# First two weight block sums of the 7-product down-projection tiles: by a plain and an adding transfer in place of VectorE

## The reference

```python
def squared_relu_mlp(n, w_up, w_down):
    return jnp.square(jax.nn.relu(n @ w_up)) @ w_down
```

## Time and profile before

| | us |
|---|---|
| median of 3 runs | 946.07 (945.78 to 946.14) |
| the profiled execution, whole | 946.75 |
| its span, first to last instruction | 944.8 |
| TensorE busy | 935.6 |
| VectorE busy | 712.6 |
| ScalarE busy | 595.3 |
| GpSimd busy | 36.2 |

### The profile page before, as it was taken

How to read it: one execution, slowest core, us unless ns; L and a number is a source line. 1 busy time by engine, 2 the same in 40 slices (tenths; PEclk the granted TensorE clock), 3 DMA queues, 4 the chain that set the end, 5 groups by cost and what they waited for, 6 DMA issues and landing times.

```text
span 944.8 us, 14583 instructions
## 1 busy us (share of the span) xinstructions
PE 935.6 (99%) x5944; PEld 832.5 (88%) x5944; DVE 712.6 (75%) x1037; ACT 595.3 (63%) x869; POOL 36.2 (4%) x15
## 2 busy tenths in 40 slices
PE   8999999999999999999999999999999999999997
PEld 7888888888888888888888888999999999999886
DVE  4997747777988867747777988876468789898643
ACT  7676548888655658838888655734555596555532
POOL 0011250000000000020000000000000000000000
PEclk9999999999999999999999999999999999999999
DMA  8554235555565552535554565454544436555541
GB/s 300 222 183 173 91 134 179 183 200 197 181 220 192 178 209 91 178 136 182 191 207 179 183 218 205 163 191 166 179 165 161 166 134 246 179 179 184 193 158 44
DMA packets 25345, 168.22 MB, mean 178 GB/s; under 512 B 2816, under 2 KB 3904, under 8 KB 5568
## 3 DMA queue, kind: packets, MB, share of 16 engines
q1 hardware_dynamic: 24848, 166.84, 49.5%
q10 hardware_dynamic: 432, 0.46, 0.2%
HBM read 166.24 MB, written 1.05 MB: 177 GB/s over the span
## 4 chain that ended last, share of the span: by engine, by line
PE 94%; DVE 3%; ACT 1%; DMA 1%; issue 1%; SPq 0%; DVEq 0%
PE bank L724 23%; PE bank L725 23%; PE bank L726 23%; PE bank L833 12%; PE bank L837 6%; PE bank L752 1%; DMA raw<-w_stream 1%; DVE wlo L1997 0%; PE bank L887 0%; PE bank L1106 0%; PE bank L891 0%; PE bank L895 0%; PE bank L1240 0%; PE bank L1132 0%; PE bank L1114 0%
## 5 line engine op out<-in xcount | busy, mean ns | idle before, releaser
L1997 DVE TENSOR_TENSOR wlo<-raw,whi 128x2048 fp32r<-128x2048 f32 (+2 forms) x133 | 296.8, 2232 | 131.2 <-ACT whi L1340 131.0
L1340 ACT ACTIVATE whi<-raw 128x2048 fp32r<-128x2048 f32 (+1 forms) x139 | 264.7, 1905 | 100.2 <-PE bank L726 97.7
L833 PE MATMUL bank<-nhl,whi 128*128 128x512 f32 x512 | 124.0, 392 | 0.0
L833 PEld LDWEIGHTS bank<-nhl,whi 128*128 128x128 f32 x512 | 94.0, 188 | 18.8 <-issue 0.7
L724 PE MATMUL bank<-mhi,whi 128*128 128x258 f32 x384 | 108.5, 282 | 0.1
L725 PE MATMUL bank<-mlo,whi 128*128 128x258 f32 x384 | 108.3, 282 | 0.0
L726 PE MATMUL bank<-mhi,wlo 128*128 128x258 f32 x384 | 108.2, 282 | 0.0
L724 PE MATMUL bank<-nhl,whi 128*128 128x258 f32 (+3 forms) x320 | 92.2, 288 | 0.0
L725 PE MATMUL bank<-nhl,whi 128*128 128x258 f32 (+3 forms) x320 | 91.4, 286 | 0.0
L726 PE MATMUL bank<-nhl,wlo 128*128 128x258 f32 (+3 forms) x320 | 90.5, 283 | 0.0
L724 PEld LDWEIGHTS bank<-mhi,whi 128*128 128x128 f32 x384 | 72.5, 189 | 0.4 <-issue 0.2
(11 more groups left out here) (389 smaller groups left out, 1914.3 us busy)
## 6 DMA issues: line engine op xcount, KB each, us to landing
raw<-w_stream SPq DMA_DIRECT2D x154, 1024.0 KB, 4.8
h<-x_rows SPq DMA_DIRECT2D x4, 256.0 KB, 5.1
raw<-w_stream SPq DMA_DIRECT2D x2, 512.0 KB, 6.7
cst<-consts SPq DMA_DIRECT2D x1, 832.0 KB, 6.3
e<-g_post SPq DMA_DIRECT2D x1, 512.0 KB, 6.7
out_rows<-e SPq DMA_DIRECT2D x2, 256.0 KB, 2.0
raw<-w_stream SPq DMA_DIRECT2D x1, 352.0 KB, 10.0
vec<-vectors SPq DMA_DIRECT2D x1, 258.5 KB, 9.5
```

The lines of the kernel that those rows point to most:

```text
L833: return pe.matmul(us[c].t[:, :], w[:, k, c * P:c * P + P].hi, nboth[:, k, :], start=k == 0, stop=k == 7)
L1340: act.activation(whi[j][:, 0:n], raw[j][:, 0:n], ACT.Copy).then_inc(s_hi.up(i))
L1997: dve.tensor_tensor(wlo[j][:, 0:m], raw[j][:, 0:m], whi[j][:, 0:m].bitcast(F32), ALU.subtract).then_inc(s_lod.up(i))
```

## The change

The first two weight sums no longer come from VectorE. SyncE issues two plain transfers of B12 (256 KB each, HBM to SBUF) into both halves of the tile, and when they have landed GpSimd issues one transfer of 512 KB (B11 and B22) that adds to what stands there (`accum_op=ALU.add`). So the tile holds B11 + B12 and B12 + B22, where it was B12 - B11 and B22 - B12. The other signs are made up for: in the two adds of `combined` into the second tile, in two of the row sums, and in `seven_2` at the end, each a subtract for an add or the reverse. The number and shape of VectorE's other instructions and all matmuls stay.

The tile of the first two sums is now double: fills q = 0, 2, 4, 6 go to the place of `inval` and `gmask` in `cst`, fills q = 1, 3, 5 to the old `TX[0]`. The second tile, `T24`, stays single. A fill of q >= 2 may start when the sums of q - 2 have been read (`s_ts` and TL's part 0); that of q = 0 waits for the first up-projection bank, that of q = 1 for the last. SyncE does the two plain transfers (`right_block`) just ahead of the stage of the same weight tile (for q = 1, just behind it). GpSimd's adding transfers (`block_sums`) stand in its loop over the tiles. `combined` on VectorE and `combined_hi` on ScalarE wait for their landing (`t13_ready`).

```diff
-        TX = [at(f"tr{i}", 1024, o_nhl + 4096 * i) for i in range(2)]
+        o_inval = CST["inval"][0]
+        T13 = [cst[:, o_inval:o_inval + 1024], at("tr0", 1024, o_nhl)]
+        T24 = at("tr1", 1024, o_nhl + 4096)
...
+        def fill(l, q):
+            return len(SEVEN[q % 2::2]) * l + q // 2 + 1
+
+        def t13_ready(l, q):
+            return s_t13[q % 2], 16 * fill(l, q)
+
+        def t_sums(l, q):
+            return T13[q % 2], T24
...
-                    on.wait_ge(*s_ts.at(l, q, part))
+                    on.wait_ge(*(s_ts.at(l, q) if part else t13_ready(l, q)))
...
-                    act.activation(TH[part], TX[part], ACT.Copy).then_inc(s_thi.up(l, q, part))
+                    act.activation(TH[part], t_sums(l, q)[part], ACT.Copy).then_inc(s_thi.up(l, q, part))
...
             def combined(l, it):
                 q, i = SEVEN.index(it), DOWN[l] + it
-                r = raw[i % NSLOT]
-                right, above = r.rearrange("p (k c n) -> p k c n", k=2, c=2)[:, :, 1, :], r[:, 0:1024].rearrange("p (k n) -> p k n", k=2)
+                r, t1 = raw[i % NSLOT], t_sums(l, q)[0][:, 0:512]
                 on.wait_ge(s_raw[i % NSLOT], 16 * (i // NSLOT + 1))
+                on.wait_ge(*t13_ready(l, q))
                 if q:
                     on.wait_ge(*s_tlo.at(l, q - 1, 1))
-                dve.tensor_tensor(TX[0].rearrange("p (k n) -> p k n", k=2), right, above, ALU.subtract).then_inc(s_ts.up(l, q, 0))
-                on.wait_ge(*s_ts.at(l, q, 0))
-                dve.tensor_tensor(TX[1][:, 0:512], r[:, 1536:2048], TX[0][:, 0:512], ALU.subtract).then_inc(own.up())
+                dve.tensor_tensor(T24[:, 0:512], r[:, 1536:2048], t1, ALU.add).then_inc(own.up())
                 on.wait_ge(*own.last())
-                dve.tensor_tensor(TX[1][:, 512:1024], r[:, 1024:1536], TX[1][:, 0:512], ALU.subtract).then_inc(s_ts.up(l, q, 1))
+                dve.tensor_tensor(T24[:, 512:1024], r[:, 1024:1536], T24[:, 0:512], ALU.add).then_inc(s_ts.up(l, q))
...
-                dve.tensor_tensor(EX[3], EX[1], p5.t[:, :], ALU.add).then_inc(s_ex.up(l))
-                dve.tensor_tensor(EX[0], EX[2], p5.t[:, :], ALU.add).then_inc(p5.free)
+                dve.tensor_tensor(EX[3], p5.t[:, :], EX[1], ALU.subtract).then_inc(s_ex.up(l))
+                dve.tensor_tensor(EX[0], p5.t[:, :], EX[2], ALU.subtract).then_inc(p5.free)
...
-                    dve.tensor_tensor(s1, a21, a22, ALU.add).then_inc(own.up())
+                    dve.tensor_tensor(s1, a21, a22, ALU.subtract).then_inc(own.up())
...
-                    dve.tensor_tensor(s4, a12, s2, ALU.subtract).then_inc(s_as.up(l, q))
+                    dve.tensor_tensor(s4, a12, s2, ALU.add).then_inc(s_as.up(l, q))
...
+            def block_sums(l, q):
+                t = t_sums(l, q)[0].rearrange("p (k n) -> p k n", k=2)
+                i = DOWN[l] + SEVEN[q]
+                corner = W[starts[i]:starts[i + 1]].rearrange("(p k n) -> p k n", p=P, k=4)[:, 0:4:3, :]
+                on.wait_ge(s_t12[q % 2], 32 * fill(l, q))
+                pool.dma_start(t, corner, accum_op=ALU.add).then_inc(s_t13[q % 2], 16)
...
+                if seven_at(i):
+                    block_sums(*seven_at(i))
...
+            def right_block(l, q):
+                t = t_sums(l, q)[0].rearrange("p (k n) -> p k n", k=2)
+                i = DOWN[l] + SEVEN[q]
+                b = W[starts[i]:starts[i + 1]].rearrange("(p n) -> p n", p=P)
+                if q < 2:
+                    on.wait_ge(*use["up", l, 15 * q, q].done())
+                else:
+                    on.wait_ge(*s_ts.at(l, q - 2))
+                    on.wait_ge(*s_tlo.at(l, q - 2, 0))
+                for k in range(2):
+                    sp.dma_start(t[:, k, :], b[:, 512:1024]).then_inc(s_t12[q % 2], 16)
...
+                if i - 1 in (DOWN[0] + SEVEN[1], DOWN[1] + SEVEN[1]):
+                    right_block(*seven_at(i - 1))
+                if seven_at(i) and seven_at(i)[1] != 1:
+                    right_block(*seven_at(i))
```

More of the change, by code:

```diff
@@ L682, in block_kernel @@
         s_as, s_ashi, s_aslo = (sig(n, grid(2, len(SEVEN))) for n in ("as", "ashi", "aslo"))
-        s_ts, s_thi, s_tlo = (sig(n, grid(2, len(SEVEN), 2)) for n in ("ts", "thi", "tlo"))
+        s_ts = sig("ts", grid(2, len(SEVEN)))
+        s_thi, s_tlo = (sig(n, grid(2, len(SEVEN), 2)) for n in ("thi", "tlo"))
+        s_t12, s_t13 = ([sem(f"s_{n}_{i}") for i in range(2)] for n in ("t12", "t13"))
+        def fill(l, q):
[4 more added lines that the diff above has]
+            return T13[q % 2], T24
         s_ex = sig("ex", range(2))
@@ L2341, in combined_lo @@
                     on.wait_ge(*s_thi.at(l, q, part))
-                    dve.tensor_tensor(TL[part], TX[part], TH[part].bitcast(F32), ALU.subtract).then_inc(s_tlo.up(l, q, part))
+                    dve.tensor_tensor(TL[part], t_sums(l, q)[part], TH[part].bitcast(F32), ALU.subtract).then_inc(s_tlo.up(l, q, part))
             def down_lo(l, it):
@@ L2869, in stage @@
                         if seven_at(i - NSLOT):
-                            on.wait_ge(*s_ts.at(*seven_at(i - NSLOT), 1))
+                            on.wait_ge(*s_ts.at(*seven_at(i - NSLOT)))
                         if cuts[i - NSLOT]:
```

## The result

| | before | after |
|---|---|---|
| median of the runs beside each other | 946.0 us (945.51 to 946.38, 6 runs) | 962.71 us (961.07 to 964.18, 6 runs) |
| the profiled execution, whole | 946.75 | 961.07 |
| its span | 944.8 | 959.2 |
| VectorE busy | 712.6 | 693.8 |

The ratio is 1.0175, with a 95% interval of 1.0164 to 1.0186: the kernel became 1.75% slower. The forecast, 946.1 us and a range up to 952.0, was wrong. The profiled execution of the changed kernel is the fastest of its six, 1.6 us under their median.

The account below looks back on a forecast made before the run. TensorE was taken as the bound, busy 935.6 of 944.8 us, so VectorE's relief gains 0 and every added transfer cost is 0: 946.75 + 0 profiled, 946.1 us on the median's scale; 8-in-10 range 945.3 to 952.0 us.

Parts of the forecast that it names:

- Bound and gain: Down-projections: TensorE never waits, so taking 17.1 us from VectorE gains 0, at most 0.15 us at each layer.
- Signs: Row sums and `seven_2`: a subtract changed into an add is the same instruction and costs nothing.
- SyncE's queue: 28 plain transfers, some 0.33 us each to issue; weight tile 13 goes out 2.4 us later; cost 0.
- the fixed cost of a new queue: GpSimd's own queue, setting up or closing: bounds 0 and +1.95 us, taken as 0.
- The work of the adding transfer: On the DMA engines: 3.0 us per transfer, twice the plain price, bounds 1.5 and 5.9 us; cost 0.
- The DMA share: Sign of being right: DMA share near 0.85 to 0.95 in the pairs of tiles.
- Tile 13: Tightest fill: signal 280.08 us, landing some 292 us; VectorE waits some 0.5 us, TensorE loses nothing, 2.5 us in hand.
- the first rival: Late fills at tile 13 in both layers, TensorE waiting on `tl`: 948, 952.7 or 961 us by adding price; chance 0.25.
- the latency of one fill: Plain issue, landing, GpSimd's issue, landing: 9.4 us unloaded, against some 14 us for tiles 6 to 12; cost 0.
- with nothing beside: One fill's latency without other transfers: 0.7 + (1.85 + 1.5) + 0.5 + (1.85 + 3.0) = 9.4 us.
- the prediction's own sum of 8.9 to 10.4 us of work in 10.2 us: DMA engines' work per pair at lower and middle adding price; at the middle just full, 0.2 us late per pair.
- the 11 us said to be in hand: Weight tile 10: 5.3 us before anything waits and 5.8 more before TensorE does, covering late transfers.

Follow-up runs that it names:

- the run with two places in layer 1 only: The changed kernel with a third place for the first two sums in layer 0, layer 1 still with two: 953.87 us, ratio 1.0092.
- the run with three of seven fills: The changed kernel with only tiles 2, 6 and 10 filled by transfers in one place, the other fills by VectorE: 950.03 us, ratio 1.0052.
- the kernel with adding transfers alone: The changed kernel with plain pairs for the first two fills only; all 14 adding transfers add to the sums standing there: 945.74 us, ratio 0.9999.

## Why the prediction was wrong

What held, by its own steps:

- Bound and gain. TensorE paces; VectorE fell by 18.8 us (17.1 expected) and gave nothing. The runs without a too short circle all measure 945.7 to 946.1 us.
- Signs, SyncE's queue, the fixed cost of a new queue: 0 as said (945.74 us with both queues in use).
- The work of the adding transfer: 3.0 us taken, 3.15 measured. The rule of the Trainium skill (Collectives: The Full Stack, Part 3), two sources on one ring, gave the same 3.0 us. The trace agrees with the doubling (3.15 against 1.48 us for a plain one) and doesn't show the reason. The DMA share was forecast as 0.85 to 0.95 and is 0.86.
- Tile 13, which I called the tight one, isn't in layer 0 (302.59 us, no wait): by then TensorE is so late that its fill has time. In layer 1 it is, by 1.54 us of VectorE's, and TensorE waits for its TL (0.92 us), the very sign that was named for the first rival.

What failed is "the latency of one fill", in two ways.

First, the size. 9.4 us "with nothing beside" stood for tiles 6 to 12 and was compared with the 14 us between signal and `combined`; 14 against 9.4 looked like enough. Measured from signal to sums: 20.5 us. The terms:

| term | taken | measured |
|---|---|---|
| plain pair, signal to GpSimd's start | 4.05 us | 7.4 and 8.5 us |
| of the next line, GpSimd's issue | 0.5 us | 1.20 us |
| adding transfer, from the start of its issue to landing | 5.35 us | 7.8 us in the middle, 11.7 and 13.0 in this circle |

At an engine share of 0.86 there is no "nothing beside". I did load the transfer with a neighbour, but for tile 13 alone, and then only by one weight tile; the prediction's own sum of 8.9 to 10.4 us of work in 10.2 us said that every fill runs beside the stream. Work per pair was asked for throughput and never for latency.

Second, the form. Each fill was held against its own need, once, as if its signal stood fixed at the time of before. But the signal of fill q+2 hangs on the reading of fill q. The test is a circle: reading 4.3 us + fill against 20.4 us per place. At 9.4 us it closes (13.7); at 20.5 us it doesn't (24.8), and what it lacks is not lost once but again at every fill. That is why TensorE's waits grow from 1.73 to 4.15 us along layer 0. And of the 11 us said to be in hand only the 5.8 us between `wlo` and TensorE stand behind a fill; the other 5.3 us lie between a weight tile's landing and `combined`, which itself waits for the fill. The first half add of tile 8 starts 7.2 us later than before (272.19 against 265.02 us), and that is more than 5.8.

The first rival (0.25) had the mechanism, late fills, but named only tile 13, where some 3 of the 15.0 us arose, and hung on the wrong quantity: the price of the add, not latency. At its real price, twice the plain, the rival said "nothing lost". No step had a price for what idleness costs TensorE afterwards, 1.6 us in each layer at half clock.

The traces also show which order makes a late fill hurt. Most of TensorE's waits are for `wlo`, which stands behind the wait for the fill in VectorE's program; the sums themselves are wanted nine matmuls, 2 us, later. No run forms `wlo` first, so what that would win isn't known.

Layer 1 lost less than layer 0 (6.56 against 8.47 us) with the same code; in the run with two places in layer 1 only it lost 7.5. Its circle of `tr` was 25.0 us and then 21.2 (538.55, 563.50, 584.71), where layer 0's was 24.6 and 24.8. Why the second was shorter stays open, and so does where the 3 us go in the slower executions of the run with three of seven fills.

## What to carry to other kernels

Where a buffer is refilled by steps that each wait for the last, add up the whole circle, reading included, with durations as they are under the load that the change makes, and compare it with (number of places) x (pace of the consumer). If it is longer, the shortfall comes back at each fill; here one more place removed it at no measurable cost, and faster transfers only help by what they shorten the circle. Steps of different places that one engine waits for in order form a circle of their own. And before work is taken from an engine, ask whether anything ever waits for that engine.

## What the runs showed of the hardware

- An adding transfer of 512 KB in rows of 2 KB takes 3.15 us of all 16 engines, about twice what a plain one of the same size takes (1.48 us, in rows of 4 KB).
- GpSimd needs 1.20 us to issue it, 0.72 us for that plain one; SyncE needs 0.33 us for a weight tile.
- Two queues that both have work share by number of rows, not by bytes (42 to 43, 65 to 65), so the queue with 8 KB rows gets most of the bytes (0.24 against 0.09 MB).
- How long an adding transfer takes from issue to its first row goes with what the other queue is doing then. In the changed kernel the one issued at 249.19 us has rows in 251 to 252 us, with VectorE busy all the while; the one issued at 260.37 us has none before 264 us. Here are the windows 251 to 252 and 262 to 263 us (packets, MB, share):

```profile
q0 software_dynamic: 35, 0.07, 56.8%
q1 hardware_dynamic: 3, 0.01, 2.0%
```

```profile
q1 hardware_dynamic: 54, 0.43, 102.6%
```

- The one issued at 283.94 us has no row until 288 us, though the other queue's share is down to 66% and 60% in the two us before. In the kernel with adding transfers alone, one issued at 279.86 us has rows by 281 to 282 us. So full engines alone don't explain the wait; the cause stays open. The windows 288 to 289 and 281 to 282 us:

```profile
q0 software_dynamic: 18, 0.04, 19.9%
```

```profile
q0 software_dynamic: 7, 0.01, 14.8%
```

- After 4.15 and after 2.02 us of idleness TensorE's granted clock was 0.53 and 0.50 over 3.4 us (1.2 GHz, the lower of its two levels), which cost 1.6 us on top of the wait; after 1.73 and 1.15 us it stayed at 1.00.
